# Sharing the first stage's scaled inputs and weight remainders between VectorE and GpSimd in a two-block transformer kernel

## What is computed

```python
mods = (silu(c) @ w_ada + b_ada).reshape(B, 9, 1, 1024)
sh1, sc1, gt1, ... = [mods[:, i] for i in range(9)]
h = rmsnorm(x, g_pre[0]) * (1 + sc1) + sh1        # rmsnorm: x * rsqrt(mean(x*x) + eps) * g
x = x + 0.5 * gt1 * rmsnorm(swiglu(h, w_gu1, w_dn1), g_post[0])
```

## Time and profile before

| | us |
|---|---|
| median of 3 runs (lowest, highest) | 2566.95 (2566.61, 2572.87) |
| the profiled execution, its own time | 2567.48 |
| its span, first to last instruction | 2565.6 |
| PE busy | 2536.2 (99%) |
| DVE busy | 1137.4 (44%) |
| ACT busy | 1033.8 (40%) |
| POOL busy | 1049.2 (41%) |

### The profile page before, as it was taken

How to read it: one execution, slowest core, us unless ns; L and a number is a source line. 1 busy time by engine, 2 the same in 40 slices (tenths; PEclk the granted TensorE clock), 3 DMA queues, 4 the chain that set the end, 5 groups by cost and what they waited for, 6 DMA issues and landing times.

```text
span 2565.6 us, 35545 instructions
## 1 busy us (share of the span) xinstructions
PE 2536.2 (99%) x12666; PEld 2112.8 (82%) x12666; DVE 1137.4 (44%) x2238; ACT 1033.8 (40%) x1681; POOL 1049.2 (41%) x464
## 2 busy tenths in 40 slices
PE   9999999999999999999999999999999999999998
PEld 7888888887887888888889888888777678888887
DVE  7444336765444145644315544224555455322212
ACT  5222237455555234332334322224565554322321
POOL 0444454342232444544455544453123335244443
PEclk9999999999999999999999999999999999999999
DMA  7455532122222333555532554333112223233332
GB/s 298 148 191 193 189 123 85 60 81 84 98 82 83 107 98 115 188 192 190 168 124 88 198 190 145 103 125 108 50 57 78 87 82 115 66 98 98 96 102 98
DMA packets 78282, 313.11 MB, mean 122 GB/s; under 512 B 9040, under 2 KB 11728, under 8 KB 68720
## 3 DMA queue, kind: packets, MB, share of 16 engines
q1 hardware_dynamic: 65376, 238.09, 28.1%
q10 hardware_dynamic: 12816, 73.80, 8.1%
HBM read 309.72 MB, written 2.13 MB: 122 GB/s over the span
## 4 chain that ended last, share of the span: by engine, by line
PE 93%; DVE 4%; ACT 2%; issue 1%; DMA 0%; POOL 0%; DVEq 0%; ACTq 0%
PE bank L2045 26%; PE bank L2047 25%; PE bank L2046 25%; PE bank L2097 2%; PE bank L2099 2%; PE bank L2098 2%; PE bank L2480 1%; PE bank L2396 1%; PE bank L2488 1%; PE bank L2369 1%; ACT h_hi L666 0%; PE bank L2567 0%; PE pair L2560 0%; PE pair L2381 0%; DVE h_lo L1295 0%
## 5 line engine op out<-in xcount | busy, mean ns | idle before, releaser
L586 POOL TENSOR_TENSOR w_lo<-raw,w_hi 128x1024 fp32r<-128x1024 f32 x412 | 1011.1, 2456 | 1431.9 <-ACT w_hi L625 1431.8
L625 ACT ACTIVATE w_hi<-raw 128x1024 fp32r<-128x1024 f32 x420 | 443.4, 1059 | 1049.9 <-PE bank L2047 1014.4
L2045 PE MATMUL bank<-h_hi,w_hi 128*128 128x512 f32 x2064 | 819.2, 397 | 2.2 <-DVE kw_lo_b L1732 2.2
L2047 PE MATMUL bank<-h_hi,w_lo 128*128 128x512 f32 x2064 | 804.5, 390 | 0.0
L2046 PE MATMUL bank<-h_lo,w_hi 128*128 128x512 f32 x2064 | 803.8, 389 | 0.0
L2045 PEld LDWEIGHTS bank<-h_hi,w_hi 128*128 128x128 f32 x2064 | 388.3, 188 | 91.1 <-issue 12.5
L2047 PEld LDWEIGHTS bank<-h_hi,w_lo 128*128 128x128 f32 x2064 | 387.7, 188 | 82.1
L2046 PEld LDWEIGHTS bank<-h_lo,w_hi 128*128 128x128 f32 x2064 | 388.3, 188 | 77.5 <-issue 1.0
L1446 DVE TENSOR_TENSOR prod<-bank,rstd 128x512 f32<-128x512 f32 x87 | 60.1, 691 | 427.8 <-PE bank L2047 417.0
L2045 PE MATMUL bank<-act_hi,w_hi 128*128 128x512 f32 x616 | 239.6, 389 | 0.0
L2046 PE MATMUL bank<-act_lo,w_hi 128*128 128x512 f32 x616 | 239.6, 389 | 0.0
(11 more groups left out here) (484 smaller groups left out, 3103.0 us busy)
## 6 DMA issues: line engine op xcount, KB each, us to landing
raw<-slabs_dram SPq DMA_DIRECT2D x420, 512.0 KB, 3.5
adaw<-ada_dram ACTq DMA_DIRECT2D x62, 1024.0 KB, 6.8
ada<-ada_dram SPq DMA_DIRECT2D x8, 1024.0 KB, 20.3
x<-xt_dram SPq DMA_DIRECT2D x4, 512.0 KB, 5.7
adaw<-ada_dram SPq DMA_DIRECT2D x2, 1024.0 KB, 23.7
fneg<-fneg_scratch ACTq DMA_DIRECT2D x4, 512.0 KB, 3.8
sq<-fneg_scratch ACTq DMA_DIRECT2D x4, 512.0 KB, 3.8
w<-w_dram SPq DMA_DIRECT2D x1, 2048.0 KB, 8.0
```

The lines of the kernel that those rows point to most:

```text
L586: nc.gpsimd.tensor_tensor(wl[s][:], raw[s][:], wh[s][:], ALU.subtract).then_inc(lo_done, 1)
L625: nc.scalar.activation(wh[s][:], raw[s][:], ACT.Copy).then_inc(hi_done, 1)
L2045: MM(out, wh[s][:, k], a, start=first and j == 0, stop=False)
L2047: ins = MM(out, wl[s][:, k], a, start=False, stop=end and j == len(tiles) - 1)
```

## The change

POOL gets products 1 to 7 of xr = x * rstd and the weight remainders 4 and 5 of the first stage. DVE keeps product 0 and remainders 0 to 3, 6 and 7, and makes remainder 0 before it waits for rstd instead of behind product 0. POOL begins when xr_done is 1, that is behind DVE's product 0, and makes remainders 4 and 5 between products 3 and 4, when lo_done is 4. The first product of K-tile 2's modulation now stands ahead of h_low(1). DVE waits for lo_done at 6 before remainder 6, so that the count stays in order.

```diff
@@ gpsimd
+            def scaled_x(n):
+
+                nc.gpsimd.tensor_tensor(xr[:, n], x[:, n], rstd[:], ALU.mult).then_inc(xr_done, 1)
+            pool.wait_ge(x_std, 5)
+            pool.wait_ge(xr_done, 1)
+            for n in range(1, 4):
+                scaled_x(n)
+            pool.wait_ge(lo_done, 4)
+            low(4)
+            low(5)
+            for n in range(4, KT):
+                scaled_x(n)
             pool.wait_ge(lo_done, AHEAD + len(ONCE))
@@ vector
-            def scaled_x(n):
-
-                V.tensor_tensor(xr[:, n], x[:, n], rstd[:], ALU.mult).then_inc(xr_done, 1)
-
@@ vector, the list
             mods(0, 1)
             set_pre(0)
+            low(0)
             dve.wait_ge(x_std, 5)
-            scaled_x(0)
-            low(0)
-            scaled_x(1)
+            V.tensor_tensor(xr[:, 0], x[:, 0], rstd[:], ALU.mult).then_inc(xr_done, 1)
             low(1)
             h_low(0)
             low(2)
@@
             set_pre(1)
-            low(4)
-            low(5)
+            mods(2, 0)
             h_low(1)
-            scaled_x(2)
-            for z in range(2):
-                mods(2, z)
+            mods(2, 1)
             set_pre(2)
             for n in range(2, KT - 1):
-                scaled_x(n + 1)
                 mods(n + 1, 0)
                 h_low(n)
                 mods(n + 1, 1)
                 set_pre(n + 1)
+            dve.wait_ge(lo_done, 6)
             low(ONCE[0])
```

## The result

The changed kernel takes 2573.17 us (median of 10 runs, 2571.46 to 2577.35) against 2567.94 us for the kernel before beside it (10 runs, 2566.23 to 2572.87): ratio 1.0021, 95% interval 1.0012 to 1.0030. That is 5.2 us slower, clear of noise but inside the 0.3% that the prediction called the same. The profiled execution took 2571.72 us with a span of 2569.8 us.

What follows compares the result with a forecast made beforehand. PE bounds the kernel (2536.2 of 2565.6 us busy), so only its head stalls count: +4.6 us from turns, +5.4 with the low clock, 2567.48 + 5.4 = 2572.9 us (2572.3 against the median), range 2567.5 to 2576.3.

Steps and rivals of the forecast that it cites:

- A delay reaches the end: Head to end of kernel: PE is 99% busy afterwards, so a delay there passes on one to one.
- Exclusion between operations with two SBUF inputs: Head, DVE beside POOL: such operations alternate, small ones too; w*silu_c stands still 2.2 us beside a POOL remainder.
- The third pattern: DVE's list: a row of operations without a gap keeps POOL out, from a 5.24 us POOL row, 2.8 over need.
- rival 1: From 22.85, between remainders 2 and 3: POOL wins every boundary between DVE operations; +7.5 us, +9.6 with low clock; chance 0.17.
- the schedule: Head, DVE and POOL turns laid out: K-tile 1 at 34.3 or 34.9, h_lo 2 at 38.7, K-tile 4 at 47.85; +4.6 us.
- The low clock: PE after its standstills, about 5.2 and 2.4 us: matmuls at 0.43 us instead of 0.23; loss +5.4 to +7.5.
- The middle case: Low level until about 3 us into K-tile 1, seven matmuls: K-tile 1 ends at 40.4, K-tile 2 at 44.5; +5.4 us.
- Remainder 0 ahead of the norm: DVE's idle 1.36 us before 17.30: it fits at 15.94 to 17.1, delays nothing; first matmul 0.3 us earlier.
- The signs: New profile's head: remainder 1 at about 19.3, w*silu_c rows of 2.4 and 3.4 us, PE idle some 5 us before slab 4.
- The estimate of 1.12 us: A 128x512 product on POOL, by proportion from the skill's 4497 ns for 2048 columns; the forecast itself took 1.25 us.

Runs made afterwards that it cites:

- e2: Against the kernel before: only the seven products go to POOL, remainders 4 and 5 stay on DVE, remainder 0 behind product 0; 2574.13 us, ratio 1.0028.
- e3: Against the kernel before: only remainders 4 and 5 go to POOL, all products stay on DVE; 2570.88 us, ratio 1.0014.
- e5: The kernel before with the first stage's w*silu_c replaced by a sum over w (one SBUF input), as control; 2567.40 us, ratio 0.9996.
- e6: The changed kernel with the first stage's w*silu_c replaced by the same sum as in e5; 2570.97 us, ratio 1.0012 to the kernel before.
- e9: e2 with DVE waiting for w_hi 5 ahead of set_pre 1, so no wait stands between set_pre 1 and remainders 4 and 5; 2574.94 us, 1.0029.
- e7: The changed kernel with 18 small PE matmuls ahead of slab 4's wait and 14 ahead of slab 5's in K-tile 0; 2575.69 us, ratio 1.0029.
- e8: The kernel before with remainder 0 ahead of the norm and 12 small PE matmuls ahead of slab 4's wait; 2566.15 us, ratio 0.9992.
- e11: The changed kernel, but POOL takes remainder 5 only when set_pre 1 is done; 2572.70 us, ratio 1.0019.

## Why the prediction held, and where its steps did not

The time was right: +5.4 us forecast, +5.2 measured in the medians and +5.4 at K-tile 3. That it came so near is luck in part, as the steps show:

- **A delay reaches the end.** Right: the offset is +5.4 at K-tile 3 and at 351.40. The profiled span ends at only +4.2, since the offset changes by up to 1.7 us at a few places later on. At one the clock is seen to differ. Stretch 440 to 460 of the kernel before, then of the changed one:

```profile
440.00:460.00 20.00, 17.55 (x87) 14.21 (x86) 17.91 (x34) 7.79 (x11) 5.33 (x2) 0.91 0.09 27
```

```profile
440.00:460.00 20.00, 17.32 (x102) 14.40 (x101) 19.43 (x46) 12.20 (x19) 5.56 (x3) 1.00 0.18 54
```

- **Exclusion between operations with two SBUF inputs, small ones too.** Right, shown by e2, e3 and the pair e5 and e6. A turn of a 128x512 product on POOL costs DVE 1.1 us, of a 128x1024 remainder 2.1 (the rows of 2.32 and 3.35 us less the 1.21 of the operation alone; taken: 1.25 and 2.3).
- **The third pattern, "a row of DVE operations without a gap keeps POOL out", is the step that failed.** POOL's product 3 got in between remainders 2 and 3 (the row of 4.25 us), and a product between set_pre 1 and the next w*silu_c (2.30 us at 30.67); e9 shows it with no wait in the program, behind a short operation. So in this respect rival 1's order held. Its price of +7.5 did not: it had a product of POOL's in front of each step of set_pre 1, and remainder 5 ending at 32.15, where it ended at 30.6 and only one product followed, behind set_pre 1.
- **The order of turns** therefore came out different from the schedule: product 3 was done at 22.96 (17.36 + 5.60) instead of 26.4, so remainder 4 was ready when DVE read its accumulator at 25.1, and remainder 5 got in ahead of set_pre 1, not behind the next product. Slab 5 could start at 30.7 instead of 33.6, and h_lo 1 set K-tile 1 at 33.64, which I had at 34.3 to 34.9. On DVE's side two things nearly cancelled by h_lo 2 (done at 39.26, forecast 38.7): the list up to its end was 22.7 us against the forecast's 21.4, and it began 0.8 us earlier than the 17.30 that I had carried over, by the norm of that execution.
- **The low clock.** The middle case was right in its outcome: K-tile 2 at 40.46 (forecast 40.4), K-tile 3 at 44.55 (forecast 44.5), both set by PE itself and not by h_lo. The size was not: K-tile 1 had twelve matmuls at the low level where I took seven, 6.8 us instead of 5.5, and began 1.3 us earlier than my 34.9. e7 puts its net share at 0.7 to 1.0 us; the forecast's own sums had 0.8 (5.4 less 4.6).
- **Remainder 0 ahead of the norm "delays nothing".** Nearly: in the changed kernel's profile PE began to spread the norm 0.5 us earlier and took 1.16 us instead of 2.08 for it (granted clock from 14.5 to 16: 0.78, before 0.50),

```profile
14.09 1.16 PE L2603 MATMUL pair<-ident,small 128*128 128x128 f32 x8 [0.64 <-DVE small L2000]
```

so rstd was there at 15.88, and remainder 0 held product 0 up until 16.53. It costs at most 0.65 us in such an execution and takes 1.14 out of the list; with the late norm of e8 the list to h_lo 2 is 0.8 us shorter.
- **The signs.** POOL's rows, the long w*silu_c rows and the set_pre row above 1 us came as listed. Remainder 1 did not wait until 19.3: it ran at 17.13 in its 1.22 us, since the norm was early and w_hi 1 was there; with the late norm of e11 it took 2.24 us from 18.52. PE stood still for 2.4 us ahead of slab 4, not for 5, and K-tiles 2 and 3 did not wait for h_lo.

## What to carry to other kernels

Before moving elementwise work from VectorE to GpSimd, count the SBUF inputs of what VectorE will run beside it: with two on each side they took turns here, one whole operation at a time, and a product that takes 0.60 us of VectorE's list came back as 1.1 us of waiting, even for an operation on a single column. Only what lay under VectorE's waits for another engine, or beside operations with one SBUF input, was free to move. And before reordering a list that waits for another engine, note which operations fill that wait: what fills it costs nothing where it stands. Last, before comparing the starts of single profiles, look when their common input arrived, here the norm: it moved by up to 1.7 us with no edit that explains it.

## What was not expected

- A sum over 128x1024 with one SBUF input ran beside POOL at full length on both sides (2.33 us for two, 4.69 us for POOL's two), while an addition on one column waited 2.2 us.
- POOL gets in between DVE operations of 128x1024 (remainders 2 and 3 of the changed kernel), and between one on one column and one of 128x1024 with no wait between them (e9), yet in the kernel before an operation of POOL's took 5.24 us at 461.71 beside DVE operations of 128x128 and 128x256. Whether short operations are treated differently stays open.
- POOL's 128x512 product took 1.27 us at the least, alone (shortest/median/longest in ns below; the longer ones include turns). The estimate of 1.12 us, by proportion from the 4497 ns of the Trainium skill (GPSIMD Engine Reference, 3.1 Elementwise), was too low; the line through this kernel's own rows gave 1.30.

```profile
L596 POOL TENSOR_TENSOR xr<-x,rstd x7: 1274/2112/2267, 17.4 to 36.3; 128x512 f32<-128x512 f32 x7
```
